# Two-layer trunk on one core: modulation in four column groups, context tile scored ahead of the latents

## What is computed

```python
def modulation(cond, w, b):                      # cond: c_ctx for the context, c for the latents
    m = jax.nn.silu(cond) @ w + b                # w: (1024, 6144) for each of 2 layers
    return jnp.split(m[:, None, :], 6, axis=-1)  # shift, scale, gate; twice

def peer(h, w_q, keys, u_tab, v_tab):            # for each tile xb of 128 tokens
    q = (xb @ w_q).reshape(BLOCK, PEER_HEADS, D_QUERY)            # 8 heads, 256
    s1 = jnp.einsum('thd,hnd->thn', q[..., :half], keys[0])       # 128 scores
    s2 = jnp.einsum('thd,hnd->thn', q[..., half:], keys[1])
    ...                                          # the best 16 of 16x16 pairs of each head
    g = jax.nn.softmax(sv, axis=-1)
    act = jax.nn.gelu(jnp.einsum('thkd,td->thk', u_tab[eidx], xb), approximate=False)
    return jnp.einsum('thk,thkd->td', g * act, v_tab[eidx])
```

## Time and profile before

| | |
|---|---|
| median of 3 runs | 5359.71 us (5347.23 to 5366.09) |
| profiled execution, its own time | 5375.3 us |
| its span | 5373.5 us |
| granted clock of TensorE, mean | 0.808 |
| busy: PE, DVE, POOL, ACT | 3638.8, 2816.2, 2833.3, 712.8 us |
| DMA over the span | 1560.49 MB, mean 290 GB/s |
| modulation | 20 to 209 us |
| mixer of layer 0 | 209 to 1231 us |
| trunk | 1231 us to the end |

### The profile page before, as it was taken

How to read it: one execution, slowest core, us unless ns; L and a number is a source line. 1 busy time by engine, 2 the same in 40 slices (tenths; PEclk the granted TensorE clock), 3 DMA queues, 4 the chain that set the end, 5 groups by cost and what they waited for, 6 DMA issues and landing times. The chain is left out here.

```text
span 5373.5 us, 55987 instructions
## 1 busy us (share of the span) xinstructions
PE 3638.8 (68%) x20670; PEld 1616.0 (30%) x20670; DVE 2816.2 (52%) x6912; ACT 712.8 (13%) x1806; POOL 2833.3 (53%) x2725
## 2 busy tenths in 40 slices
PE   7798569968526666666656767756766666666666
PEld 1255258834300013223213313413421421220011
DVE  0124834434976556655455655655656656556520
ACT  0103512201100001200001201310310310000000
POOL 0000011101677766766666775665676666677765
PEclk9896679989767768878878878877887887776789
DMA  8420000014999999999999999999999999999998
GB/s 296 141 59 11 9 22 1 0 40 142 333 343 359 369 367 379 357 357 386 373 366 383 341 366 382 362 357 383 347 374 376 334 378 373 352 369 368 373 361 328
DMA packets 467641, 1560.49 MB, mean 290 GB/s; under 512 B 57849, under 2 KB 76650, under 8 KB 467178
## 3 DMA queue, kind: packets, MB, share of 16 engines
q0 software_dynamic: 368640, 1342.34, 66.4%
q1 hardware_dynamic: 98648, 215.48, 11.3%
q10 hardware_dynamic: 152, 0.14, 0.0%
HBM read 1554.66 MB, written 3.11 MB: 290 GB/s over the span
## 5 line engine op out<-in xcount | busy, mean ns | idle before, releaser
L2044 PE MATMUL t_ps<-t_vring,t_wz 128*32 128x512 f32 x4864 | 1744.7, 837 | 1135.5 <-DMA t_vring<-in_peer_v,t_eidT 987.6
L1570 DVE SCALAR_TENSOR_TENSOR t_uring<-t_uring,t_hring 128x1024 f32<-128x1024 f32 x1024 | 1254.7, 1225 | 1207.4 <-DMA t_uring<-in_peer_u,t_eidx 1090.3
L1449 POOL DMA_INDIRECT t_vring<-in_peer_v,t_eidT x1216 | 1347.5, 1108 | 796.3 <-PE t_ps L2044 441.1
L1435 POOL DMA_INDIRECT t_uring<-in_peer_u,t_eidx x1280 | 1358.7, 1061 | 528.6 <-issue 374.4
L2044 PEld LDWEIGHTS t_ps<-t_vring,t_wz 128*32 128x32 f32 x4864 | 262.7, 128 | 2359.1 <-DMA t_vring<-in_peer_v,t_eidT 1806.4
L1570 DVE SCALAR_TENSOR_TENSOR t_uring<-t_uring,t_early 128x1024 f32<-128x1024 f32 x256 | 312.8, 1223 | 170.1 <-DMA t_uring<-in_peer_u,t_eidx 157.9
L905 POOL COPY scp_vb<-ev_u 64x256 f32 x8 | 3.9, 489 | 699.6 <-DVE scp_vb L1030 687.7
L1797 ACT ACTIVATE t_early<-ident,vec 128x128 f32<-128x128 f32 x775 | 256.3, 392 | 313.3 <-PE t_ps L1940 164.8
L1922 PE MATMUL t_ps<-t_hT,t_wg 128*128 128x128 f32 x1280 | 179.2, 305 | 48.5 <-DMA t_wg<-in_cv_w_pw 48.5
L1940 PE MATMUL t_ps<-t_early 128*128 128x128 f32 x1550 | 198.9, 287 | 15.1 <-remote 6.5
L1940 PEld LDWEIGHTS t_ps<-t_early 128*128 128x128 f32 x1550 | 187.6, 200 | 58.1 <-issue 57.7
(11 more groups left out here) (407 smaller groups left out, 4036.7 us busy)
## 6 DMA issues: line engine op xcount, KB each, us to landing
mod_wring<-in_mod_w SPq DMA_DIRECT2D x24, 2048.0 KB, 8.4
t_wq<-in_peer_w_q SPq DMA_DIRECT2D x96, 512.0 KB
t_wg<-in_cv_w_pw SPq DMA_DIRECT2D x80, 512.0 KB
t_uring<-in_peer_u,t_eidx POOLq DMA_INDIRECT x1280
t_wq<-in_cv_w_pw SPq DMA_DIRECT2D x40, 512.0 KB
t_vring<-in_peer_v,t_eidT POOLq DMA_INDIRECT x1216
t_pair<-modrows SPq DMA_DIRECT2D x25, 512.0 KB
in_wring<-in_ab_w_in SPq DMA_DIRECT2D x17, 512.0 KB, 4.0
```

Of the source, the lines that this page charges most:

```text
L1435: pool.indirect_dma_start(uring[:, slot(n), :], None, u_tab, bass.IndirectOffsetOnAxis(ap=eidx[:, s % 2, r:r + 1], axis=0)).then_inc(u_in[ ...
L1449: pool.indirect_dma_start(vring[:, slot(n), :], None, v_tab, index).then_inc(v_in[slot(n)], 16)
L1570: V.scalar_tensor_tensor(uring[:, n % R, :], uring[:, n % R, :], 1.0, h_of(j), ALU.mult, ALU.mult, accum_out=dots[:, j % 2, r:r + 1]).then ...
L2044: last = nc.tensor.matmul(ps[32 * g:32 * g + 32, j % 2, a * 512:(a + 1) * 512], wz[:, first:first + 32], ring[:, n % R, a * 512:(a + 1) * ...
```

## The change

**Modulation.** The chunks go in 6 groups of 4. The four chunks of a group are multiplied into four column groups of the array: chunk r writes partitions 32r and 32r + 1, and the order on PE is by k, then by r. The weights are laid out anew in DRAM, so that a chunk is one block whose partition has a run of 16 KB; the ring holds two groups. Biases and norm weights are loaded to the same four places of the partitions (12 DMAs of ACT in place of 2). DVE adds the bias chunk by chunk, and applies the norm's weights right behind the group. Four stores replace one.

```diff
-        wring = sb("mod_wring", [P, RING, KD, 512])
+        wring = sb("mod_wring", [P, 2, 4, KD * 512])
...
+        lanes = lambda r: slice(32 * r, 32 * r + 2)
...
-                            sp.wait_ge(chunk_done, i * RING + (layer * NCH + r + 1))
-                            sp.dma_start(wring[:, r], w[:, :, bass.ds((i * RING + r) * 512, 512)]).then_inc(w_in[r], 16)
+                for g in range(GROUPS):
+                    if g >= 2:
+                        sp.wait_ge(group_done, g - 1)
+                    for r in range(4):
+                        layer, n = chunk(g, r)
+                        sp.dma_start(wring[:, g % 2, r, :], io["mod_w"][layer, n]).then_inc(w_in[g % 2][r], 16)
...
+                for g in range(GROUPS):
+                    if g >= 2:
+                        pe.wait_ge(row_done, 4 * (g - 1))
+                    for k in range(KD):
+                        for r in range(4):
+                            if k == 0:
+                                pe.wait_ge(w_in[g % 2][r], 16 * (g // 2 + 1))
+                            last = nc.tensor.matmul(ps[lanes(r), g % 2, :], csil[:, k, :], wring[:, g % 2, r, k * 512:(k + 1) * 512],
+                                                    start=(k == 0), stop=(k == KD - 1))
+                    last.then_inc(group_done, 1)
```

```diff
-                for b in range(NC):
-                    load_q(0, b, b)
+                for n in range(Q0):
+                    load_q(0, n % NC, n)
...
-                    dve.wait_ge(S["s_copied"], (2 * (hd + 1)) if j < NT else 2 * PH * (j - NT + 1) + 2 * (hd + 1))
+                    dve.wait_ge(S["s_copied"], (0 if j == 0 else NC if j < NT else Q0 + NC * (j - NT)) + 2 * (hd + 1))
...
+                for b in range(NC + 1):
+                    if b == 13:
+                        Side(exponents(0)).run(0)
+                    if b < NC:
+                        act.wait_ge(S["q_done"], NC + b + 1)
+                        nc.scalar.copy(qT0[:, b % 2, :], banks[:, 4 + b % 2, :]).then_inc(S["q_copied"], 1)
...
+                def score_context():
+                    for b in range(NC + 1):
+                        if b < NC:
+                            if b >= 2:
+                                pe.wait_ge(S["q_copied"], b - 1)
+                            queries(b, 0, P, banks[:, 6 + b % 2, 0:P])
+                        if b:
+                            pe.wait_ge(S["q_copied"], b)
+                            if b >= 3:
+                                pe.wait_ge(S["s_copied"], b - 2)
+                            nc.tensor.matmul(banks[:, 4 + (b - 1) % 2, 0:P], qT1[:, (b - 1) % 2, :], keysT[:, b - 1, :],
+                                             start=True, stop=True).then_inc(S["s_done"], 1)
...
-                pe.wait_ge(S["s_copied"], NC)
+                turn(0, 2)
+                pe.wait_ge(S["hT_done"], 2)
+                pe.wait_ge(S["keys_in"], 16)
+                score_context()
+                turn(2, 2 * NT)
+                pe.wait_ge(S["hT_done"], 2 * NT)
+                score_latents()
+                pe.wait_ge(S["s_copied"], Q0)
```

More of the change, by code:

```diff
@@ L188, in _ @@
             def _(pe):
-                pe.sem_inc(chunk_done, RING)
                 pe.wait_ge(silu_done, 1)
[L191 to L200, removed]
+                for g in range(GROUPS):
+                    if g >= 2:
+                        pe.wait_ge(row_done, 4 * (g - 1))
+                    for k in range(KD):
+                        for r in range(4):
+                            if k == 0:
[3 more added lines that the diff above has]
+                    last.then_inc(group_done, 1)
@@ L202, in _ @@
             @block.vector
             def _(dve):
[L204 to L217, removed]
+                dve.wait_ge(small_in, 16 * 12)
+                for g in range(GROUPS):
+                    dve.wait_ge(group_done, g + 1)
+                    for r in range(4):
+                        nc.vector.tensor_tensor(rows[lanes(r), g, :], ps[lanes(r), g % 2, :], bias[lanes(r), g, :], ALU.add).then_inc(row_done, 1)
+                    for r in range(4):
+                        layer, n = chunk(g, r)
+                        if (g, r) in scales:
+                            dve.wait_ge(row_done, 4 * (g + 1))
+                            row = rows[lanes(r), g, :]
+                            nc.vector.scalar_tensor_tensor(row, row, 1.0, normg[lanes(r), layer, n // 6, :], ALU.add, ALU.mult).then_inc(scaled, 1)
@@ L1873, in _, with turn @@
             def _(pe):
-                def queries(b):
-                    pe.wait_ge(wq_in[b % 2], 16 * (b // 2 + 1))
-                    if b >= 2:
-                        pe.wait_ge(S["s_copied"], b - 1)
+                def turn(first, last):
+                    for n in range(first, last):
+                        t, b = n // 2, n % 2
+                        pe.wait_ge(S["h_done"], t + 1)
+                        if n >= 4:
+                            pe.wait_ge(S["hT_done"], n - 3)
+                        for k in range(4):
+                            done = nc.tensor.transpose(banks[:, n % 4, k * P:(k + 1) * P], h_of(t)[:, (4 * b + k) * P:(4 * b + k + 1) * P], ident[:])
+                        done.then_inc(S["turned"], 1)
@@ L1878, in queries @@
+                def queries(n, first, width, out):
+                    pe.wait_ge(wq_in[n % 2], 16 * (n // 2 + 1))
                     for k in range(KD):
-                        nc.tensor.matmul(ps[:, 2 + b % 2, SQ:512], wq[:, b % 2, k, :], hT0[:, k, 0:T_CTX], start=(k == 0), stop=(k == KD - 1))
-                        last = nc.tensor.matmul(ps[:, 2 + b % 2, 512:1024], wq[:, b % 2, k, :], hT0[:, k, T_CTX:T], start=(k == 0), stop=(k == KD - 1))
+                        last = nc.tensor.matmul(out, wq[:, n % 2, k, :], hT0[:, k, first:first + width], start=(k == 0), stop=(k == KD - 1))
@@ new lines, in score_latents @@
+                def score_latents():
+                    for b in range(NC + 1):
+                        if b < NC:
+                            if b >= 2:
+                                pe.wait_ge(S["q_copied"], NC + b - 1)
+                            queries(NC + b, T_CTX, T_LAT, banks[:, 4 + b % 2, :])
+                        if b:
+                            c = b - 1
+                            pe.wait_ge(S["q_copied"], NC + b)
+                            if b >= 3:
+                                pe.wait_ge(S["s_copied"], NC + b - 2)
+                            for t in range(NT - 1):
+                                last = nc.tensor.matmul(banks[:, c % 2, t * P:(t + 1) * P], qT0[:, c % 2, t * P:(t + 1) * P],
+                                                        keysT[:, c, :], start=True, stop=True)
+                            last.then_inc(S["s_done"], 1)
@@ L2140 @@
         laid[n] = np.ascontiguousarray(w).reshape(-1, cols, P, KD * P)
+    w = laid["mod_w"].reshape(DEPTH, P, KD, 6 * D // 512, 512).transpose(0, 3, 1, 2, 4)
+    laid["mod_w"] = np.ascontiguousarray(w).reshape(DEPTH, -1, P, KD * 512)
     keys = laid["peer_keys"].transpose(0, 4, 2, 1, 3)
```

122 lines of the change are left out of this document (55 added, 67 removed).

## The result

The kernel after takes **5292.86 us** (median of 4 runs, 5290.93 to 5303.63) beside 5361.6 us for the kernel before (4 runs): ratio 0.988, 95% interval 0.9857 to 0.9904. That is 69 us less, where 65 were forecast, and 5292.9 where 5295 stood. The profiled execution took 5292.12 us, its span 5290.3.

The account below looks back on a forecast made before the run. The prediction took PE to bound the modulation and DVE slot 0 of the trunk. Modulation -35 and trunk -30 (-16.5 - 17.4 + 4) make -65 us: 5295 us from the median 5359.7, range 5270 to 5345.

Parts of the forecast that it names:

- What bounded the kernel: PE bounds the modulation, DVE bounds slot 0 at the trunk's start, bytes bound the long stage, which the change leaves alone.
- The load: Modulation: DMA engines set the pace at 372 GB/s, last chunk landed at 158 us; modulation -35 us in all.
- the last group: Modulation's tail: 15 waves left when the last chunk lands, PE beginning at half clock, 8.1 us.
- the store's 1.5 us: Modulation's end: four stores in place of one, with three more issues of about 0.3 us, win 1.5 us.
- First choice: Start of the trunk: DVE's first choice comes at about 1260 us in place of 1276.5, -16.5 us.
- Waits for scores: Slot 0 of the trunk: DVE's waits for ACT's copies of scores go, -17.4 us.
- Contention: Slot 0: the second loading of w_q, 8.4 MB, competes with the gathers, +4 us.
- The exponentials: Slot 0's gates: ACT reaches block 13 ahead of DVE's subtraction and waits 6 us; DVE waits for nothing, 0 us.
- exponentials late: Rival, slot 0: slow context blocks make ACT late for the exponentials, DVE waits 14 us, 5309 us; chance 0.10.
- Long runs are slow: Rival, modulation: 16 KB runs load slowly, 5330 to 5402 us; chances 0.14 (about 300 GB/s), 0.10 (under 255).
- The DMA takes the trunk's gain: Rival, slot 0: the second w_q loading costs 23 us in place of 4, 5314 us; chance 0.06.
- Columns don't run side by side: Rival, modulation: a group takes 27.5 us on PE, 10 us lost where 33.5 were won, 5339 us; chance 0.02.

Follow-up runs that it names:

- one_column: Kernel after, but its modulation has the ring of four chunks, loops and single column group of the kernel before, keeping the new weight layout: 5372.76 us, ratio 0.9968.
- again: The kernel after, unchanged, measured once more: 5291.85 us, ratio 0.9868 to the kernel before.
- exp11: Kernel after with ACT's exponentials two blocks earlier in the latents' scoring, ahead of block 11 in place of 13: 5282.85 us, ratio 0.9847.
- short_runs: Kernel after with the modulation's weights in their old layout, so runs of 2 KB in place of 16 KB: 5330.67 us, ratio 0.9900.
- no_reload: exp11 with the first layer's second loading of w_q cut to a thirty-second part (latents' right scores left out): 5310.62 us, ratio 0.9848.
- again_b: The kernel after, unchanged, measured a third time in a later set of runs: 5323.84 us, ratio 0.9872 to the kernel before.
- trunk_only: The new trunk with the modulation of the kernel before: 5372.74 us, ratio 0.9959 to the kernel before.
- chunk_outer: Kernel after with PE's two modulation loops exchanged, so all passes of a chunk go to one column group before the next: 5331.75 us, ratio 0.9899.
- exp12: Kernel after with ACT's exponentials one block earlier in the latents' scoring, ahead of block 12 in place of 13: 5293.82 us, ratio 0.9857.
- exp_last: Kernel after with ACT's exponentials behind all of the latents' scoring, their place before the change: 5322.73 us, ratio 0.9923.

## Why the prediction was right, and where its steps were not

**What bounded the kernel.** Right in both places. one_column shows that PE's single column group held the load at 302 GB/s, and in slot 0, which I had given to DVE, 12.0 us of DVE's wait taken out (again to exp11) shorten the slot by 9.3.

**The load** was the largest mis-sized term, -35 us forecast and -46.9 measured. I took 372 GB/s, from windows of the kernel before. PE was busy for 15.0 of 15 us where 360 was read, and both windows had 2 KB runs, which short_runs brought at 409 GB/s once PE had time to spare. The load held 431, and PE's last group found its last chunk at 143.1 us, not 158: 15 us. The Trainium skill ("DMA: Bandwidth & Descriptors", Bandwidth) gives 425 GB/s for 16 MB with the neighbouring core idle, a figure that I had set aside; this trace bears it out with 427 to 431. The 207 to 214 GB/s of the Trainium skill (the same page, Latency and other measured facts) are for copies between HBM tensors whose rows lie 512 KB or 4 MB + 4 KB apart, which I left unsaid; they did not carry over to a load into SBUF from blocks that lie in one piece. The other terms of the modulation went the other way and were small: the last group 9.0 us for 8.1 (its first passes came 0.85 us apart for five steps, not four), DVE 4.3 us for 3.9, and the store's 1.5 us did not come (5.5 us from DVE's end to the next phase, 5.3 before): the issues of the four stores alone took 2.75 us, where I had 0.3 for each one more. Sum: -15 + 0.9 + 0.4 + 1.7 = -12, the difference between -35 and -47.

**First choice.** -16.5 forecast, -17.1 measured (34.1 to 17.0 us).

**Waits for scores.** -17.4 forecast; they went entirely.

**Contention.** +4 forecast, 3.8 to 5.5 measured by no_reload.

**The exponentials.** This step failed: 0 forecast, 8.9 us measured (12.0 and 12.5 in the repeats). I had ACT at block 13 143 us behind the first dot's start, DVE's subtraction at 149 (the sum as I wrote it gives 148.3), and a slack of about 9 us. In the trace ACT's table load is 150.6 us behind the first dot's start (1225.7 us), and the subtraction 140.7. ACT is 7.6 us late, DVE 8.3 us early, of which 4 are contention that I had charged ahead of the gates. Together that is some 16 us against the slack of 9, and ACT's table load and exponentials, 1.6 us, which I had left out, come on top: 8.9 us.

ACT's lateness has two parts, which the timeline of PE tells apart (turning of the latents' tiles, and their first queries):

```profile
1263.99 1.04 PE L1896 MATMUL t_ps<-ident,t_early 128*128 128x128 f32 x8
1264.87 2.78 PE L1896 MATMUL t_ps<-ident,t_hring 128*128 128x128 f32 x24
1268.69 7.13 PE L1902 MATMUL t_ps<-t_vring,t_wq 128*128 128x512 f32 x16 [1.05 <-ACT t_vring L1850]
```

The latents' scoring begins 43.0 us behind the first dot's start, where I had 39: 4 us. The turning took the 5 us that I gave it, so the context's blocks are what was late. From there to the table load it is 107.5 us for 13 blocks, where I had 104: 3.5 us. So the rival "exponentials late" named the wait that came (14 us) and, in part, its cause: the context did run slower, though not at its start (the first choice was on time) and by less than the 23 us that it reckoned. This part also moves the wait from run to run: the latents' scoring begins 40.0 us behind the first dot in one_column, 43.0 in the kernel after, 46.3 in again, 46.7 in again_b and 48.7 in trunk_only, and DVE waits in this order 7.2, 8.9, 12.0, 12.5 and 13.8 us. Two estimates of 140 to 150 us each had been subtracted to give a margin of 9.

**The sum.** Modulation -46.9, first choice -17.1, slot 0 -8.6 (forecast -13.4) make -73 us in the traces, whose whole spans differ by 83, and 69 was measured between medians. That 65 stood in the forecast is a little luck: 12 us of gain too few in the modulation and 9 us of wait that the sum put at nothing nearly cancel.

**The rivals.** *Long runs are slow*, 0.24 in all, was false: 13.0 and 18.5 GB/s for an engine came from lone DMAs, one of them a store; in the stream an engine has 431/16 = 26.9. Why a lone one shows less was not tried. I gave such rows too much weight as a rate. *The DMA takes the trunk's gain*: false, 3.8 to 5.5 us and not 23. *Columns don't run side by side*: false: the weight loads come four at a time, and chunk_outer's steps read as some overlap even where the order hardly asks for it.

**Left open.** Why a latents' block takes 8.3 us and not 8.0 was not tried. It isn't the gathers' contention, since all 16 take 132.4 us in every trace of the new trunk. What makes the context's blocks end up to 10 us later than reckoned was not tried either; in again PE waits for loads of `w_q` between them, up to 3.2 us at a time. Whether the 4 to 5 us of the second loading fall ahead of the gates or behind them isn't shown.

## What to carry to other kernels

In this kernel the matmuls with two rows of output had used one column group of four; four side by side turned a stage bound by PE into one bound by the DMA engines, and the layout only paid once that was done (one_column: nothing; behind the column groups: 8 us). A rate read while another engine set the pace, or from a lone DMA, is a poor measure of what a stream will do. Where an in-order engine has a step placed by hand in a periodic loop, the margin is the difference of two long times: place it a period or two earlier than the sum says, where waiting is free; here, one period later lengthened slot 0 by 8.6 us (exp12 to again), and two periods early cost nothing.

## What the runs showed beyond this

- Passes for different column groups overlap where the program changes group, with no interleaving in the program: 16 passes in 12 steps of 0.43 us (chunk_outer), which reads as four in a row beside the four before them.
- Runs of 16 KB came at 430 GB/s with a DMA share of 1.01, runs of 2 KB at 409 with 1.05.
- In the traces, a stall of DVE is partly paid back in the waits for gathered rows: 16.8 us more of stall, 11.6 us more of slot 0 (exp_last), though its median is 30.9 us higher.
- In the modulation after, PE idles before each group, and its granted clock averages 0.77. A group in the timeline of PE:

```profile
65.33 8.61 PE L206 MATMUL mod_ps<-mod_wring,csil 128*2 128x512 f32 x60 [3.87 <-DMA mod_wring<-in_mod_w]
```

At full clock its 60 passes, 15 steps of 0.43 us, would be 6.5 us; the 2.1 us more are those of half clock, as in the last group, where the granted clock is 0.50 from 143 to 147 us and 1.00 from 148 on. They lie on the path in the last group only.
